# Layer norm's mean and mean square on TensorE: one fp32 matmul each, or two float32r passes over an exact split

## The reference, cut to what matters

```python
u = c_val * jax.nn.sigmoid(c_gate)
u = causal_depthwise_conv(u, w_dw[l], b_dw[l])      # 31 taps per channel
u = jax.nn.silu(layer_norm(u, g_conv_ln[l], b_conv_ln[l]))

def layer_norm(x, g, b):
    mu = jnp.mean(x, axis=-1, keepdims=True)
    var = jnp.mean(jnp.square(x - mu), axis=-1, keepdims=True)
    return (x - mu) * lax.rsqrt(var + EPS) * g + b
```

## Time and profile before

| | |
|---|---|
| median of 3 runs | 1184.67 us (1183.99 to 1185.15) |
| profiled execution, span | 1182.9 us |
| PE busy | 1099.4 us, 93% |
| DVE busy | 848.3 us, 72% |
| ACT busy | 572.4 us, 48% |
| POOL busy | 319.2 us, 27% |

### The profile page before, as it was taken

One profiled execution on the slowest core, in us unless ns is written; L12 is line 12 of the kernel. 1 busy time (PEld: TensorE's weight loads), 2 busy tenths in 40 slices (PEclk: granted clock), 3 DMA queues, 4 the chain that ended last, 5 costly groups with the idle time before them and its releaser, 6 DMA issues.

```text
span 1182.9 us, 15278 instructions
## 1 busy us (share of the span) xinstructions
PE 1099.4 (93%) x5116; PEld 880.9 (74%) x5116; DVE 848.3 (72%) x1086; ACT 572.4 (48%) x730; POOL 319.2 (27%) x323
## 2 busy tenths in 40 slices
PE   5999999999997788899999899998999999999896
PEld 4988888887664556676688788887788888787784
DVE  4438999996346567666557645676999999797794
ACT  4531112122346554345423222225888888787883
POOL 3010000002083541000000000012457767665652
PEclk9999999999999998999999999998999999999998
DMA  6021123332100001000493235565999999898972
GB/s 242 1 55 38 50 89 97 98 106 90 45 35 19 1 1 36 1 1 1 121 324 88 59 117 212 204 208 185 322 355 322 315 317 308 299 320 283 325 244 34
DMA packets 115458, 176.46 MB, mean 149 GB/s; under 512 B 12331, under 2 KB 62678, under 8 KB 115414
## 3 DMA queue, kind: packets, MB, share of 16 engines
q1 hardware_dynamic: 102614, 150.69, 38.4%
q0 software_dynamic: 10432, 16.81, 6.0%
q10 hardware_dynamic: 2368, 8.41, 1.8%
HBM read 161.18 MB, written 35.65 MB: 166 GB/s over the span
## 4 chain that ended last, share of the span: by engine, by line
PE 46%; DVE 6%; DMA 6%; ACT 2%; issue 1%; ACTq 0%; DVEq 0%; POOL 0%; POOLq 0%; SPq 0%
PE pb L1573 11%; PE pb L1575 11%; PE pb L1574 11%; DMA wed_raw<-in_w_e_down 6%; PE pb L1739 4%; PE pb L1880 2%; PE pb L1803 1%; PE pb L1671 1%; PE pb L1727 1%; PE pb L1728 1%; PE pb L1726 1%; DVE prob_sums L1306 1%; ACT wgu_hi L986 1%; PE pb L1794 1%; PE pb L1866 1%
## 5 line engine op out<-in xcount | busy, mean ns | idle before, releaser
L1498 DVE TENSOR_TENSOR wgu_lo<-wgu_raw,wgu_hi 128x2048 fp32r<-128x2048 f32 x72 | 165.0, 2293 | 36.6 <-ACT wgu_hi L986 36.5
L1124 DVE SCALAR_TENSOR_TENSOR cv<-up,dwc,cv 128x1024 f32<-128x1024 f32 x120 | 154.1, 1284 | 3.7
L1573 PE MATMUL pb<-hT_hi,ws_hi 128*128 128x512 f32 x384 | 155.3, 404 | 1.3 <-ACT lnr L867 1.3
L986 ACT ACTIVATE wgu_hi<-wgu_raw 128x2048 fp32r (+1 forms) x72 | 137.8, 1916 | 31.2 <-DMA out<-x 13.5
L1575 PE MATMUL pb<-hT_hi,ws_lo 128*128 128x512 f32 x384 | 149.8, 390 | 0.0
L1574 PE MATMUL pb<-hT_lo,ws_hi 128*128 128x512 f32 x384 | 149.7, 390 | 0.0
L1573 PE MATMUL pb<-wgu_hi,hgT_hi 128*128 128x512 f32 x288 | 116.9, 406 | 1.9 <-DVE hgT_lo L1502 1.9
L1575 PE MATMUL pb<-wgu_hi,hgT_lo 128*128 128x512 f32 x288 | 113.0, 392 | 0.0
L1574 PE MATMUL pb<-wgu_lo,hgT_hi 128*128 128x512 f32 x288 | 112.4, 390 | 0.0
L726 POOL DMA_INDIRECT out<-yb,rcol x36 | 72.0, 2000 | 109.4 <-ACT yb L1047 55.4
L618 POOL TENSOR_SCALAR rs<-ss 128x1 f32<-128x1 f32 x16 | 4.2, 264 | 324.4 <-ACT h2T L946 297.5
(11 more groups left out here) (318 smaller groups left out, 2537.0 us busy)
## 6 DMA issues: line engine op xcount, KB each, us to landing
wgu_raw<-in_w_e_gate SPq DMA_DIRECT2D x32, 1024.0 KB, 8.1
wgu_raw<-in_w_e_up SPq DMA_DIRECT2D x32, 1024.0 KB, 18.4
wed_raw<-in_w_e_down SPq DMA_DIRECT2D x32, 1024.0 KB, 20.1
ws_raw<-in_w_in SPq DMA_DIRECT2D x24, 512.0 KB, 3.9
gates_kept<-gring ACTq DMA_DIRECT2D x16, 512.0 KB, 2.6
gates<-gates_kept SPq DMA_DIRECT2D x16, 512.0 KB, 7.2
xs<-in_x SPq DMA_DIRECT2D x8, 512.0 KB, 8.7
wout<-in_w_out SPq DMA_DIRECT2D x1, 4096.0 KB, 12.9
```

Source lines behind the costliest of these rows:

```text
L986: a.activation(wgu_hi[q % 2][:, :, ks, :], raw, ACT.Copy).then_inc(gu_hi, 1)
L1124: i = v.scalar_tensor_tensor(out=cv[:, c, :], in0=src, scalar=w, in1=cv[:, c, :], op0=ALU.mult, op1=ALU.add)
L1498: v.tensor_tensor(wgu_lo[q % 2][:, :, ks, :], wgu_raw[:, bass.ds((e + (SLOTS - 1)) % SLOTS, 1), :, ks, :].rearrange("p o g k f -> p (o g) ...
L1573: t_.matmul(out, w(0), m(0), start=start, stop=False)
```

## The change

The sources of the two means are split in the same manner as all other operands. `mean_w` becomes float32r (1/512 has no rest, so it needs no lo part). Of `cv`, ACT makes `ln_h` and DVE `ln_l` per channel block, in iterations 6, 11, 15 and 19 (`LN_SPLIT`), after the taps of that block are done; of the squares, ACT computes a second, rounded copy behind each `lnt`, and DVE subtracts it after its four subtractions of the mean. PE then runs 16 float32r matmuls (8 over hi, 8 over lo) for each mean. `ln_l` lies on the same bytes as `lnt`, `ln_h` on free ones. Two semaphores are merged into others to make room for the new ones (`ident_ok` into `consts`, `swt_ps` into `slot_ps`), with the same instructions as their sources.

```diff
+LN_SPLIT = (6, 11, 15, 19)
+    ln_h = place("ln_h", [P, NC, T], F32R, R2 + 16 * K)
+    ln_l = [place(f"ln_l{c}", [P, T], F32R, o) for c, o in enumerate((QTO, QTO + 4 * K, R3 + 16 * K, R3 + 20 * K))]
-    mean_w = small("mean_w", [P, P])
+    mean_w = small("mean_w", [P, P], F32R)
...
 ACT, iteration u, after unit_hi(u + 2):
+                if u in LN_SPLIT:
+                    c = LN_SPLIT.index(u)
+                    act.wait_ge(conv_done, c + 1)
+                    a.activation(ln_h[:, c, :], cv[:, c, :], ACT.Copy).then_inc(ln_hi, 1)
                 if u == LN_UNIT:
                     for c in range(NC):
                         act.wait_ge(ln_d, c + 1)
                         a.activation(lnt[c][:, :], cv[:, c, :], ACT.Square).then_inc(ln_sq, 1)
+                        a.activation(ln_h[:, c, :], cv[:, c, :], ACT.Square).then_inc(ln_hi, 1)
...
 DVE, iteration u, after the taps:
+                if u in LN_SPLIT:
+                    c = LN_SPLIT.index(u)
+                    dve.wait_ge(ln_hi, c + 1)
+                    dve.wait_ge(conv_done, c + 1)
+                    v.tensor_tensor(ln_l[c][:, :], cv[:, c, :], ln_h[:, c, :].bitcast(F32), ALU.subtract).then_inc(ln_lo, 1)
...
                     for c in range(NC):
                         v.tensor_tensor(cv[:, c, :], cv[:, c, :], banks(0, 2), ALU.subtract).then_inc(ln_d, 1)
+                    for c in range(NC):
+                        dve.wait_ge(ln_hi, NC + c + 1)
+                        dve.wait_ge(ln_sq, c + 1)
+                        v.tensor_tensor(ln_l[c][:, :], lnt[c][:, :], ln_h[:, c, :].bitcast(F32), ALU.subtract).then_inc(ln_lo, 1)
...
 PE:
                 if u == LN_UNIT:
-                    pe.wait_ge(conv_done, NC)
+                    pe.wait_ge(ln_lo, NC)
                     for f in range(2):
+                        cols = slice(f * 512, (f + 1) * 512)
                         for c in range(NC):
-                            i = t_.matmul(pb[:, f, :], mean_w[:, :], cv[:, c, f * 512:(f + 1) * 512], start=(c == 0), stop=(c == NC - 1))
+                            t_.matmul(pb[:, f, :], mean_w[:, :], ln_h[:, c, cols], start=(c == 0), stop=False)
+                            i = t_.matmul(pb[:, f, :], mean_w[:, :], ln_l[c][:, cols], start=False, stop=(c == NC - 1))
...
                     for c in range(NC):
-                        pe.wait_ge(ln_sq, c + 1)
+                        pe.wait_ge(ln_lo, NC + c + 1)
                         for f in range(2):
-                            i = t_.matmul(pb[:, 6 + f, :], mean_w[:, :], lnt[c][:, f * 512:(f + 1) * 512], start=(c == 0), stop=(c == NC - 1))
+                            cols = slice(f * 512, (f + 1) * 512)
+                            t_.matmul(pb[:, 6 + f, :], mean_w[:, :], ln_h[:, c, cols], start=(c == 0), stop=False)
+                            i = t_.matmul(pb[:, 6 + f, :], mean_w[:, :], ln_l[c][:, cols], start=False, stop=(c == NC - 1))
```

More of the change, by code:

```diff
@@ L283, in build @@
         h2_out = [sem("h2_out0"), sem("h2_out1")]
-        consts, ident_ok = sem("consts"), sem("ident_ok")
+        consts = sem("consts")
         vec_t, vec_c = sem("vec_t"), sem("vec_c")
@@ L295, in build @@
         ss3_ok, qd_ok, sin_in, sin_ok, tab_ok = [sem(n) for n in ("ss3_ok", "qd_ok", "sin_in", "sin_ok", "tab_ok")]
+        ln_hi, ln_lo = sem("ln_hi"), sem("ln_lo")
         ln_mu, ln_d, ln_sq, ln_var, ln_sd, ln_y = [sem(n) for n in ("ln_mu", "ln_d", "ln_sq", "ln_var", "ln_sd", "ln_y")]
@@ L321, in build @@
         wt_ok = sem("token_weights")
-        x1_out, bexp_ok, stok_ok, swt_ps = [sem(n) for n in ("x1_out", "block_experts", "slot_weights", "slot_weights_ps")]
+        x1_out, bexp_ok, stok_ok = [sem(n) for n in ("x1_out", "block_experts", "slot_weights")]
         x_v = x[0].rearrange("(j p) d -> j p d", p=P)
@@ L589, in _ @@
             g.affine_select(out=ident[:, :], in_=ident[:, :], compare_op=ALU.not_equal, fill=1.0, base=0,
-                            pattern=[[-1, P]], channel_multiplier=1).then_inc(ident_ok, 1)
-            g.memset(mean_w[:, :], 1.0 / CW)
+                            pattern=[[-1, P]], channel_multiplier=1).then_inc(consts, 1)
+            g.memset(mean_w[:, :].bitcast(F32), 1.0 / CW)
             g.memset(eps[:, :], EPS)
@@ L1019, in _ @@
             last = act.value_load(ntrip_i[0:1, 0:1], min_val=NE // SLOTS - 1, max_val=MAXB // SLOTS - 1)
-            act.wait_ge(swt_ps, 1)
+            act.wait_ge(slot_ps, 2)
             def middle_hi(nth, to):
@@ L1079, in _ @@
             row_scale(1)
-            dve.wait_ge(consts, 1)
+            dve.wait_ge(consts, 2)
             dve.wait_ge(small_in, 16 * 13)
@@ L1510, in _ @@
             expert_lo(0, 1, 0, e0)
-            dve.wait_ge(swt_ps, 1)
+            dve.wait_ge(slot_ps, 2)
             v.tensor_copy(swt[:, :], pb[:, 7, 0:NBT]).then_inc(stok_ok, 1)
@@ L1580, in scaled_T @@
                 if j == 0:
-                    pe.wait_ge(ident_ok, 1)
+                    pe.wait_ge(consts, 1)
                 if j >= 2:
@@ L1588, in _ @@
             scaled_T(0)
-            pe.wait_ge(consts, 1)
+            pe.wait_ge(consts, 2)
             pe.wait_ge(small_in, 16 * 13)
@@ L1866, in _ @@
                 i = t_.matmul(pb[:, 7, 0:NBT], ohp[:, m, :], ohbw[:, m, :], start=(m == 0), stop=(m == 2 * NTILE - 1))
-            i.then_inc(swt_ps, 1)
+            i.then_inc(slot_ps, 1)
             pe.sem_inc(y_a, 1)
```

## The result

The changed kernel took 1177.47 us in the median of 20 runs (1174.35 to 1182.27), the kernel before 1185.11 us in 20 runs beside it (1179.11 to 1190.14). The ratio is 0.9947, 95% interval 0.9934 to 0.9959: 6.3 us faster, between 4.9 and 7.8. The two medians alone differ by 7.6 us (0.9936), inside the same interval. The forecast was 5.7 us less. The executions of one kernel spread over 8 to 11 us here, wider than the three runs shown ahead of the prediction.

A forecast was written before the change was run, and what follows sets the result against it. The prediction took PE's full queue as the bound. Mean -3.23, mean square -2.92 and stall +0.42 sum to -5.73 us, so 1184.67 - 5.7 = 1178.9 us, with a range of 1177.4 to 1181.2.

The forecast's parts named there:

- The bound: From unit 0 on PE is full, so any microsecond taken off its queue moves all that follows, unless operands come later.
- Mean, gain 3.23: Mean on PE before unit 21: 16 float32r passes at 0.2267 us take 3.63 us in place of 6.86.
- rival (c): A float32r pass with `mean_w` also costs 0.429 us, so only the stall is left: 1185.1 us; chance 0.03.
- the sustained rate of 131 ns per matmul: Mean's 16 passes would take 2.1 us, saving 1.5 us more, 1177.4 us in all; the prediction did not follow it.
- Stall, cost 0.42: DVE's added pass in iteration 6 makes PE start unit 9 late, costing 0.42 us; no other unit stalls.
- 0.3 to 0.5 us of recorded idle time: Sign of being right: PE's first idle time, before unit 9, released by `ws_lo`, and none at units 10 to 20.
- Operands of the squares, cost 0: ACT's and DVE's split squares are ready during unit 21, about 14.1 us after the mean starts, with 3 us over.
- Mean square, gain 2.92, table load next late: After unit 21, PE goes on at 5.41 us in place of 8.33; ACT's square-root table load then ends last.
- `wuq`, 1.6 us of slack left: Load of `wuq`, issued after unit 23's lo part: its slack before first use falls from 4.5 to 1.6 us.
- Rival (a), the clock: PE's longer gap at the square root brings a lower clock, costing 1.7 us: 1180.6 us; chance 0.10.
- Rival (b), starving: DVE's late lo parts stall PE at three unit boundaries, 3.45 us plus 5.1 for the clock: 1187.1 us; chance 0.03.
- Rival (d), given back later: A stage behind waits for something that does not move, such as `wuq`; half the gain lost: 1181.8 us; chance 0.07.

The follow-up runs named there:

- the halves alone: Two variants of the changed kernel, splitting only the mean or only the mean square; time ratios to the kernel before 0.9989 and 0.9982.
- the doubling: Changed kernel with every float32r pass of both means done twice; time ratio to the kernel before 1.0013.
- the second trace: The changed kernel run and traced once more, unaltered; 1175.82 us in the median of 6 runs, ratio to the kernel before 0.993.
- `sq_hi_only`: Changed kernel with the mean square summed over the hi part alone (8 passes); first matmul of unit 0 to that of unit 22 248.80 us, against 248.85.
- `best`: Changed kernel with splits in iterations 12, 14, 16, 19 and gate 13's store issued behind the square root; 1176.13 us, ratio to the kernel before 0.9938.
- `split6_x3`: Changed kernel with DVE's pass in iteration 6 done three times; first matmul of unit 0 to that of unit 22 252.76 us, against 248.85.

## Why the prediction was right

**The bound.** PE full from unit 0 on, so that passes taken off its queue move all that follows: the halves alone and the doubling show it, 2.90, 2.92 and 6.89 us for 2.81, 2.92 and 6.95 expected.

**Mean, gain 3.23.** Measured 6.86 - 3.63 = 3.23. The spacing stood at 0.227 us with `mean_w`; rival (c) is out, and so is the sustained rate of 131 ns per matmul that the Trainium skill states in "TensorE: Matmul & The Clock Gate", section "Back-to-back issue gap": no float32r stream here came under 0.227 us.

**Stall, cost 0.42.** Measured 248.85 - 248.43 = 0.42 by moving the passes away (0.38 in the second trace), at the unit named and at no other. That the sum comes out to the hundredth is luck: the forecast has PE 0.34 us late at the entry and 0.08 for the first spacing, measured are 0.24 at the entry and 0.17 in the spacings behind it. One detail of what was to be seen was wrong: I named 0.3 to 0.5 us of recorded idle time there, and the timeline shows none. The ends of matmul records are modelled and overlap the next start, so a stall this short shows only in the starts (160.71 to 161.17 where 0.23 is the spacing) and in the two or three wider spacings behind.

**Operands of the squares, cost 0.** The last was forecast at 14.1 us behind the start of the mean and came at 306.12 - 291.91 = 14.2.

**Mean square, gain 2.92, table load next late.** Measured 8.33 - 5.40 = 2.93. `sq_hi_only` shows that the table load holds the root, and `best` that 0.3 us come back when it is earlier.

**`wuq`, 1.6 us of slack left.** Issued at 310.58 us, 4.2 us to landing in the changed kernel too, first used at 316.38: 1.6.

**Rival (a), the clock.** It did not come at 1.62 us of recorded idle time, in none of five traces with that gap; it did at 2.60 and 3.42. The mechanism is real and the forecast lay on the safe side of it. The rival compared lengths of gaps, and that is not enough: the gap of 1.97 us from which it took its price was followed by the fall in eight of the ten traces, and at the same length not in `split6_x3` and `sq_hi_only`, whose clock had fallen earlier. What else decides is open.

**Rival (b), starving.** Only one boundary was hit. `split6_x3` shows how its price is made: 2.5 us more of waiting cost 3.9 at unit 22 with the clock, and 2.2 some 50 us later.

**Rival (d), given back later.** The profiled pair looked like it (5.8 won, 3.1 at the end), the second trace and the runs do not: (d) left 2.9 us of gain, the two comparisons gave 6.3 and 8.3.

**Size.** 5.7 against 6.3 (4.9 to 7.8). The second comparison gave 1 - 0.993 = 0.7%, 8.3 us (5.9 to 10.8), which leaves the 5.8 of the traces just outside. Whether the stages behind unit 22 also became a little shorter on average is open; a spread of 7 us in their length hides it in ten traces. The range ahead (1177.4 to 1181.2) held the 1177.47 us by less than 0.1, which is luck: it was built on the spread of three runs (1.2 us), where twenty of the same kernel spread over 11.0 us.

## What to carry to other kernels

Where one engine's queue has no gap, count what is taken off it by start-to-start spacing, then look for what arrives second: here an activation table load took 0.3 us of 3.2 before anyone gained by it. The helpers' added passes cost nothing where their engine is ahead of the need and, where it is behind, their overhang and some tenths for the restart of the engine that waits (0.2 us of overhang cost 0.4 here), so tabulate "ready" against "wanted" for each step of a loop and put them where the slack is. For changes of less than 1% compare distances between two fixed instructions of the undisturbed part, and take a second trace before explaining a difference at the end.

## What the runs showed of the hardware that was not expected

A stall can cost more than its length at first, and part of that can come back. 2.60 us of idle time in an otherwise full stretch were followed by 4 us at a granted clock of 0.61, and 3.42 us by five at 0.50, the lower of the two levels; after 1.30 and 1.62 us the clock stayed at the upper one. Length alone does not decide it: a gap of 1.96 to 1.98 us before the queries, in all ten traces, was followed by a fall in eight and not in the two that had lost clock earlier, and `split6_x3` had 3.9 us more at unit 22 but 2.2 some 50 us later. These are two traces, and a cause was not tested. And the same program with nearly the same gaps is not always granted the same: over the same 16 us one execution had 0.68 and another 0.89.
